# Four result buffers instead of two between the experts' down projection and the scatter-add

## What is computed

```python
def moe_ffn(h, w_router, router_bias, w_gate_e, w_up_e, w_down_e, w_gate_s, w_up_s, w_down_s):
    scores = sigmoid(h @ w_router)
    _, top_idx = lax.top_k(scores + router_bias, TOP_K)            # 8 of 64 experts for each token
    top_w = top_s / sum(top_s) * ROUTE_SCALE
    routed = sum_e gates_e * (silu(xb @ w_gate_e) * (xb @ w_up_e)) @ w_down_e
    return routed.reshape(n, d) + swiglu(h, w_gate_s, w_up_s, w_down_s)
```

## Time and profile before

| | |
|---|---|
| median of 3 runs | 1139.67 us (1137.89 to 1141.78) |
| profiled execution | 1139.03 us |
| its span | 1136.4 us |
| outside the span | 2.6 us |
| mean granted TensorE clock | 0.989 |
| PE busy | 1099.9 us, 97% |
| DVE busy | 870.9 us, 77% |
| ACT busy | 727.5 us, 64% |
| POOL busy | 324.2 us, 29% |

### The profile page before, as it was taken

One profiled execution on the slowest core, in us unless ns is written; L12 is line 12 of the kernel. 1 busy time (PEld: TensorE's weight loads), 2 busy tenths in 40 slices (PEclk: granted clock), 3 DMA queues, 4 the chain that ended last, 5 costly groups with the idle time before them and its releaser, 6 DMA issues.

```text
span 1136.4 us, 18759 instructions
## 1 busy us (share of the span) xinstructions
PE 1099.9 (97%) x5682; PEld 881.9 (78%) x5682; DVE 870.9 (77%) x1383; ACT 727.5 (64%) x1282; POOL 324.2 (29%) x293
## 2 busy tenths in 40 slices
PE   7999999999999999999999999999999999999995
PEld 5888978777776477468888888888888888788884
DVE  5544376478762644569999999999999999999993
ACT  5334364544345222148888888888888788888883
POOL 0221012000000000116322543336445536533353
PEclk7999999999999999999999999999999999999998
DMA  5433312421522083639999999999999999999962
GB/s 178 140 76 112 111 38 75 149 74 39 154 88 93 1 356 115 268 134 378 389 388 380 377 363 386 387 386 382 382 362 385 364 377 370 375 382 382 377 214 35
DMA packets 69701, 284.66 MB, mean 250 GB/s; under 512 B 16611, under 2 KB 19179, under 8 KB 44700
## 3 DMA queue, kind: packets, MB, share of 16 engines
q1 hardware_dynamic: 51228, 250.50, 56.6%
q0 software_dynamic: 18432, 33.61, 12.4%
HBM read 279.79 MB, written 37.81 MB: 279 GB/s over the span
## 4 chain that ended last, share of the span: by engine, by line
PE 44%; DMA 37%; DVE 7%; issue 4%; POOL 4%; ACT 3%; POOLq 0%; SPq 0%; ACTq 0%; DVEq 0%
DMA out<-arena,idxs 34%; PE bank L1518 20%; PE bank L1687 6%; PE bank L1701 4%; PE bank L1467 2%; PE bank L1675 2%; PE bank L1661 2%; POOL turn L571 2%; DMA arena<-hn_dram,idxg 2%; DVE w_lo L1008 1%; PE bank L1657 1%; PE bank L1715 1%; ACT arena L745 1%; DVE gu_parts L1309 1%; DMA arena<-in_x 1%
## 5 line engine op out<-in xcount | busy, mean ns | idle before, releaser
L1687 PE MATMUL bank<-gu_parts,xT_parts 128*128 128x512 f32 x1280 | 339.2, 395 | 1.6 <-DVE gu_parts L1309 0.5
L1687 PEld LDWEIGHTS bank<-gu_parts,xT_parts 128*128 128x128 f32 x1280 | 235.3, 188 | 49.2 <-DVE gu_parts L1309 1.0
L1701 PE MATMUL bank<-w_lo 128*128 128x512 f32 x804 | 201.6, 399 | 0.9 <-DVE w_lo L1315 0.9
L571 POOL TENSOR_TENSOR turn<-minus_half 16x1 f32<-16x1 f32 x128 | 90.3, 705 | 346.0 <-DMA out<-arena,idxs 287.2
L1701 PEld LDWEIGHTS bank<-w_lo 128*128 128x128 f32 x804 | 146.3, 188 | 29.7 <-DVE w_lo L1315 1.1
L1518 PE MATMUL bank<-w_hi,hT_hi 128*128 128x512 f32 (+1 forms) x320 | 126.0, 394 | 2.5 <-DVE w_lo L1008 1.5
L1518 PE MATMUL bank<-w_hi,hT_lo 128*128 128x512 f32 (+1 forms) x320 | 122.7, 384 | 0.0
L1518 PE MATMUL bank<-w_lo,hT_hi 128*128 128x512 f32 (+1 forms) x320 | 122.7, 383 | 0.0
L581 POOL DMA_INDIRECT out<-arena,idxs x64 | 112.2, 1753 | 27.8 <-issue 24.9
L1309 DVE TENSOR_TENSOR gu_parts<-arena_x,gu_parts 128x1024 fp32r<-128x1024 f32 x96 | 116.6, 1215 | 1.2 <-ACT gu_parts L873 1.2
L1309 DVE TENSOR_TENSOR gu_parts<-arena,gu_parts 128x1024 fp32r<-128x1024 f32 x96 | 116.5, 1213 | 0.3 <-ACT gu_parts L873 0.3
(11 more groups left out here) (196 smaller groups left out, 1949.8 us busy)
## 6 DMA issues: line engine op xcount, KB each, us to landing
arena<-in_w_gate_e SPq DMA_DIRECT2D x32, 1024.0 KB
arena<-in_w_up_e SPq DMA_DIRECT2D x32, 1024.0 KB, 12.1
arena<-in_w_down_e SPq DMA_DIRECT2D x32, 1024.0 KB
arena_x<-in_w_gate_e SPq DMA_DIRECT2D x32, 1024.0 KB
arena_x<-in_w_up_e SPq DMA_DIRECT2D x32, 1024.0 KB, 12.1
arena_x<-in_w_down_e SPq DMA_DIRECT2D x32, 1024.0 KB
arena<-in_w_in SPq DMA_DIRECT2D x14, 1024.0 KB, 5.4
arena<-in_w_gate SPq DMA_DIRECT2D x8, 1024.0 KB, 5.8
```

Source lines behind the costliest of these rows:

```text
L571: nc.gpsimd.tensor_tensor(turn[:], minus_half[0:16, 0:1], minus_half[0:16, 0:1], ALU.add).then_inc(turns, 1)
L1687: last = nc.tensor.matmul(out_, a[:, PER * c + j, :], b[c][:, :, j, :], start=(c == 0 and j == 0 and i == 0), stop=(c == CHUNKS - 1 and j ...
L1701: last = nc.tensor.matmul(psY[h][0:rows, :], midT[n][a][:, j, 0:rows], w[b][:, j, h * 512:(h + 1) * 512], start=(j == 0 and k == 0), stop= ...
```

## The change

The results get four buffers: the two at 24 and 28 KB of the arena, one at 117 KB and one at 20 KB. The place at 23 KB held `pos`, the position of each token in its expert's list, which is read through the whole loop; it moves to a tile of its own, `pos_kept`. `y_i` takes the slot k mod 4 instead of k mod 2, and before it writes, it waits for the scatters 0 to k-4 to have landed instead of 0 to k-2. `scatter_k` reads the same slot. The waits of `scatter_k` and of `keep_idx`, and the four buffers `idxs`, stay as they are.

```diff
+        pos_kept = sb("pos_kept", [P, NT * E])
...
-        y = [at(24 + 4 * i, D) for i in range(2)]
+        y = [at(k, D) for k in (24, 28, 117, 20)]
...
-        pos = at(23, NT * E).rearrange("p (t e) -> p t e", t=NT)
+        pos = pos_kept[:].rearrange("p (t e) -> p t e", t=NT)
...
                 after(pool, scattered, 16 * k)
-                scatter(u % 2, idxs[u], before, scattered)
+                scatter(u, idxs[u], before, scattered)
...
-            def y_i(it, n):
-                after(act, scattered, 16 * (it - SH - 1))
+            def y_i(it, slot):
+                after(act, scattered, 16 * (it - SH - 3))
                 for h in range(2):
                     act.wait_ge(y_psum, 2 * it + h + 1)
-                    copy_y(n, h).then_inc(y_ready, 1)
+                    copy_y(slot, h).then_inc(y_ready, 1)
...
-                y_i(it - 1, 1 - n)
+                y_i(it - 1, (slot + 3) % 4)
                 midT_i(it, n, SLOTS)
                 wd_i(it, slot)
...
-            y_i(ITEMS - 1, 1)
+            y_i(ITEMS - 1, 3)
```

## The result

The changed kernel takes 1196.82 us (median of 4 runs, 1184.20 to 1204.32) against 1139.95 us before (median of 4 runs): a ratio of 1.0465, 95% interval 1.0425 to 1.0505. It is 57 us slower where 3 us faster was forecast, far outside the range of 1132.5 to 1141.5 us. The profiled execution took 1204.32 us, with a span of 1202.0 us; it is the slowest of the four runs, so its sums of waits are at the upper end.

What follows compares the result with a forecast made beforehand. PE at 9.52 us a step and the serial scatter chain at 9.77 us were taken to bound the kernel. A chain gain of 2.3 us gave 1136.7 us, or 1137.4 against the median; forecast 1137.0 us, range 1132.5 to 1141.5 us.

Steps and rivals of the forecast that it cites:

- What bounds the kernel: Expert loop: PE could do 9.52 us a step, the serial scatter chain 9.77; PE's whole loss is 10.2 us.
- Step (1): ACT's wait in y_i: it costs ACT 24.3 us; loosening it is worth 0 to 4.7 us in PE.
- Step (2): ACT's keep_idx: its wait binds next, so ACT gains 3.1 us of slack, once, not two steps of 9.5 us.
- Step (3): Scatter chain on POOL: its rule stays, but it gains about half of PE's 4.7 us, 2.3 us.
- Step (4): Gathers behind the scatters: rows arrive later for PE, returning part of ACT's wait; hence half of 4.7 us.
- Step (5): Tail after the last result: the end follows the chain, not PE, and moves by 2.3 us.
- Step (6): pos in its own tile and slots at 117 and 20 KB: same instructions from other addresses, costed at 0.
- The second rival: Scatter chain: no effect, as scatter time depends on whether loads are pending, not on buffers; 1139 to 1140 us; chance 0.17.
- The third rival: Weight loads, asked for earlier by PE, crowd the scatters; period 9.84 us gives 1143 us, 9.87 gives 1145; chance 0.10.
- last sign of being wrong: Scatters in the loop: the forecast fails above all if their durations react to PE's timing otherwise than read; no size given.

Runs made afterwards that it cites:

- fourth run: Changed kernel with POOL issuing gather k+5 ahead of scatter k instead of behind it: 1209.00 us, ratio to before 1.0621.
- first run: Changed kernel with the result of expert k waiting for scatter k-2 again, four buffers, their places and pos_kept staying: 1137.70 us, ratio 1.0001.

## Why the prediction was wrong

*What bounds the kernel.* Right: the serial chain of scatters and PE have nearly equal paces, and the chain sets the end. The run with half of the up weights confirms the 10 us between them.

*Step (1)*, what the old wait costs: as a sum right, 24.3 us in ACT and little of it in PE, but it was read as cost alone. The wait had an effect that no row of those shows: when a scatter was late, ACT stood still, the split of the down weights was late, and the group of 3 MB was asked for later. In the trace of before, from 560 us on, the groups stand 9.52 us apart on average where ACT did not wait for a scatter in between (32 of them), and 10.02 us where it did (23, with waits of 1.06 us on average). The loads thus mostly kept their place between two scatters.

*Step (2)*, `keep_idx` binds next: right, its wait appeared, but with 70.5 us instead of a few. I took the slack of 3.1 us as something that is used once.

*Step (3)* is the one that failed, and with it the forecast: the 2.3 us that the chain was to gain are its term of the sum, and the chain lost 70 us. It said that a late scatter "meets the loads at a later and emptier point", and that the chain would gain some 2.3 us. Of how a scatter's duration depends on the loads I had a single pair of rows and a tendency, and those came from a kernel in which none of the scatters 4 to 55 stood within 1 us of the up load: in its range of places, later was shorter. As soon as ACT didn't wait, PE went on at 9.5 us a step while scatters took 10 (scatters 4 to 11 of the changed kernel), the distance grew, and they slid onto the loads, where one takes 10.2 us on average. The two traces part at scatter 11, which both issue at nearly the same time. In the kernel before ACT has just waited 1.19 us for scatter 10, and the up load comes 5.17 us behind scatter 11, which takes 8.01 us:

```profile
635.23 1.09 ACT L841 ACTIVATE arena<-bank 128x512 f32<-128x512 f32 x2 [1.19 <-DMA out<-arena,idxs]
...
635.99 1.59 POOL L581 DMA_INDIRECT out<-arena,idxs  x1 [0.38 <-issue]
...
641.16 0.38 SPq L479 DMA_DIRECT2D arena_x<-in_w_up_e  x1
```

In the changed kernel ACT does not wait there, and the up load comes 3.2 us behind the scatter of 636.42 us, which takes 11.09 us:

```profile
639.64 0.42 SPq L480 DMA_DIRECT2D arena_x<-in_w_up_e  x1
```

Behind scatter 12 it comes 0.84 us later, and there the kernel stays: `keep_idx` and the gathers then hold PE to the landing of scatters, and PE's progress sets the loads, so that these come round with the scatters at the same unfavourable place. Shown by runs are that the looser wait brings the loss (the wait alone undone), that the loads lengthen the scatters (half of the up weights), and that their place does it (late loads, with opposite signs in the two kernels). That the old wait acted by way of the loads is supported, not shown alone: delaying only the loads gives back 48 of the 57 us, and the wait at the split gives back all of them, but holds ACT too. How the drift starts and why it ends at that place is read off single traces.

*Step (4)*, gathers come back on PE: right in kind, 45.1 us instead of some 5, but a consequence only: without them (fourth run) the time was longer still.

*Step (5)*, the end follows the chain: right in kind. The chain came out 69 us later at scatter 57, the end 65.6 us.

*Step (6)*, the places at no cost: right, shown by the first run.

*The second rival* failed too: with the same loads to be carried, the mean duration of a scatter went from 8.76 to 10.12 us, so it does not hang only on whether loads are pending.

*The third rival*, to which I gave 0.10, had the right sign and the right quantity to watch, the chain's period. It was priced at 9.84 to 9.87 us, and 11.09 us came. I had held against it that a longer period would hold PE at the next wait "and so space the loads again". It does hold PE, but at a point of the step that puts the loads beside the scatter. Had I tabulated durations against the issue of the loads in the trace of before, the nine scatters with the up load 3 us or more behind them (means of 7.3 and 8.0 us in the table's last two rows) beside the 38 in the table's first row at 9.0 us would have shown that the place matters by more than the 0.07 us which the rival needed. The prediction's own last sign of being wrong, that durations of scatters react to PE's timing otherwise than read from a handful of rows, is what came.

What stays open is what makes a scatter long when 2 MB are asked for within a microsecond of it, while 1 MB of down weights beside it does little, and where the last 9 us of the run with late loads go.

## What to carry to other kernels

When two streams of transfers share the DMA engines, and one of them is a serial chain, a wait for a buffer may be what keeps them out of each other's way, as it was here. Before loosening such a wait, ask what else it delays, and lay the durations of the chain's transfers over the issue times of the other stream. Slack gained at one place of a ring of dependences need not be used just once: here it let the parts shift against each other, and the pace at the place where they came to rest decided.

## What the runs showed of the hardware

A scatter-add of an expert's rows took 7.85 us on average when the 2 MB of gate and up loads on another queue were issued 5 us or more behind it, and 10.25 us when they were issued within 1 us of it; single kernels differ from these means, as said below the table. 1 MB of down weights issued within 1 us of it, with the 2 MB at least 3 us away, left it at 8.54 us. With no weight loads beside it, it took 4.7 to 6.1 us (the last six of the changed kernel). The traffic in the slow pace was lower than in the fast one (331 GB/s from 1000 to 1050 us against 385 GB/s from 550 to 600 us of the same run), so more traffic did not go with longer transfers here. Runs of one kernel spread by 42 us (1155.48 to 1197.47), and whether that is the time at which it fell into the slow pace stays a reading.
